# Router product inside the output projection, gated embedding tile by tile, three buffers of gathered rows

## What is computed

```python
# first block, after its four mixers have given y [512, 1024]
x1 = layer_norm(alpha * x + y @ w_out)                    # output projection
logits = x1 @ router_w + router_b                         # 32 experts
top_val, top_idx = top_k(logits, 4); gate = softmax(top_val)
# each token goes to its 4 experts (clamped SwiGLU), rows sorted by expert
ffn = alpha * x1 + sum_n gate[:, n] * expert_n(x1)
# gated embedding
h = ffn + sigmoid(ffn @ ple_gate_w) * (p @ ple_proj)
x  = layer_norm(layer_norm(h))                            # ln2, then ln_emb of the second block
# second block: two layers with retention, pooling and forgetting attention, and a feed-forward part
```

## Time and profile before

| | |
|---|---|
| median of 3 runs | 3852.95 us (3851.31 to 3853.45) |
| profiled execution, its time | 3862.78 us |
| its span, first to last instruction | 3861.0 us |
| mean granted PE clock | 0.892 of full |
| PE busy | 3518.7 us (91%) |
| DVE busy | 996.7 us (26%) |
| ACT busy | 445.7 us (12%) |
| POOL busy | 33.8 us (1%) |

### The profile page before, as it was taken

One profiled execution on the slowest core, in us unless ns is written; L12 is line 12 of the kernel. 1 busy time (PEld: TensorE's weight loads), 2 busy tenths in 40 slices (PEclk: granted clock), 3 DMA queues, 4 the chain that ended last, 5 costly groups with the idle time before them and its releaser, 6 DMA issues.

```text
span 3861.0 us, 52352 instructions
## 1 busy us (share of the span) xinstructions
PE 3518.7 (91%) x21886; PEld 2013.8 (52%) x21886; DVE 996.7 (26%) x2017; ACT 445.7 (12%) x990; POOL 33.8 (1%) x37
## 2 busy tenths in 40 slices
PE   8985578699999999999689889999999879999998
PEld 3553464444444444444346455888544646588843
DVE  0245764311111111111430354100021144300002
...
DMA packets 79323, 648.77 MB, mean 168 GB/s; under 512 B 8776, under 2 KB 21720, under 8 KB 45288
## 3 DMA queue, kind: packets, MB, share of 16 engines
...
## 4 chain that ended last, share of the span: by engine, by line
PE 88%; DVE 7%; issue 2%; DMA 2%; ACT 1%; POOL 1%; DVEq 0%; ACTq 0%; POOLq 0%; SPq 0%
PE psum L879 17%; PE psum L1225 16%; PE psum L1198 11%; PE psum L956 9%; PE psum L1025 5%; PE psum L545 4%; PE psum L553 3%; PE psum L1156 2%; PE psum L1043 2%; PE psum L561 2%; PE psum L1178 2%; PE psum L1083 2%; PE psum L1094 2%; PE psum L823 1%; PE psum L977 1%
## 5 line engine op out<-in xcount | busy, mean ns | idle before, releaser
L879 PE MATMUL psum<-weight_ring,arena 128*32 128x512 f32 x6192 | 685.1, 594 | 0.0
L1225 PE MATMUL psum<-arena,weight_ring 128*128 128x264 f32 x2816 | 627.1, 385 | 1.7 <-ACT arena L1617 1.7
L1225 PEld LDWEIGHTS psum<-arena,weight_ring 128*128 128x128 f32 x2816 | 532.2, 189 | 96.3 <-ACT arena L1617 2.2
L1198 PE MATMUL psum<-weight_ring,arena 128*128 128x512 f32 x960 | 414.1, 593 | 0.0
L879 PEld LDWEIGHTS psum<-weight_ring,arena 128*32 128x32 f32 x6192 | 195.3, 110 | 419.3 <-issue 406.7
L956 PE MATMUL psum<-weight_ring,arena 128*32 128x256 f32 x6144 | 338.2, 380 | 1.1
L545 PE MATMUL psum<-arena 128*128 128x128 f32 (+5 forms) x1078 | 187.8, 320 | 149.8 <-DVE arena L2302 24.7
L1198 PEld LDWEIGHTS psum<-weight_ring,arena 128*128 128x128 f32 x960 | 181.8, 190 | 232.6 <-issue 232.6
L545 PEld LDWEIGHTS psum<-arena 128*128 128x128 f32 (+5 forms) x1078 | 139.7, 167 | 272.3 <-issue 185.3
L956 PEld LDWEIGHTS psum<-weight_ring,arena 128*32 128x32 f32 x6144 | 196.5, 110 | 135.0 <-ACT arena L1574 8.7
L2221 DVE COPY arena<-psum 128x384 f32<-128x384 f32 x32 | 17.9, 561 | 808.8 <-PE psum L545 808.8
...
## 6 DMA issues: line engine op xcount, KB each, us to landing
...
y_sorted<-arena ACTq DMA_DIRECT2D x128, 96.0 KB, 10.8
...
```

The source lines that it names most:

```text
L879: mm = pe.matmul(psum[j * GROUP:(j + 1) * GROUP, g, :], xg[:, k, g * GROUP:(g + 1) * GROUP], w[:, kk, j * 512:(j + 1) * 512], start=(k == ...
L1198: mm = pe.matmul(bank[0:SIZE[t], :], lhs(k), rhs(k), start=(k == 0), stop=(k == tiles - 1))
L1225: mm = pe.matmul(bank[:, 0:HALF], w[:, k, at:at + P], h2_t[:, k, c * HALF:(c + 1) * HALF], start=(k == 0), stop=(k == KT - 1))
```

## The change

Three edits, each on several engines.

- **Router**: the tile's transposes and its 8 products of 32 columns move into `mix_out()`: after the second half's product group of tile 1 stands the routing of tile 0, after that of tile 2 the routing of tile 1, after that of tile 3 the routings of tiles 2 and 3. Each routing waits for its own two copies. The logits go to PSUM bank 7 instead of a bank of `v_ring`, with a semaphore of their own. On ACT the copies of x1's tile t - 1 stand behind the root of tile t.
- **Gated embedding**: all weights are waited for first; PE goes tile by tile, both halves of a tile together, and turns the next tile after the first half. ACT and DVE follow that order; the two norms of a tile come after its second half.
- **Gathered rows**: three buffers (slots 0 to 2) instead of two; POOL's wait for `ffn_ready` stands before the fourth tile only.

```diff
-        given_rows = ring[:, PIECE:3 * PIECE].rearrange("p (b n d) -> p b n d", b=2, n=TOP)
+        given_rows = ring[:, 0:3 * PIECE].rearrange("p (b n d) -> p b n d", b=3, n=TOP)
...
             for t in range(TT):
                 rwkv_tile(t)
-            def transposed_rows(source, ready):
-                for t in range(TT):
-                    if ready is not None:
-                        pe.wait_ge(ready, t + 1)
-                    for half in range(2):
-                        bank = a_ring.bank(pe)
-                        for k in range(4):
-                            mm = transpose(bank[:, k * P:(k + 1) * P], source[:, t, (4 * half + k) * P:(4 * half + k + 1) * P])
-                        job = a_ring.ship(mm)
+            def transposed_tile(source, t, ready=None):
+                if ready is not None:
+                    pe.wait_ge(ready, t + 1)
+                for half in range(2):
+                    bank = a_ring.bank(pe)
+                    for k in range(4):
+                        mm = transpose(bank[:, k * P:(k + 1) * P], source[:, t, (4 * half + k) * P:(4 * half + k + 1) * P])
+                    job = a_ring.ship(mm)
                 return job
+            def route_tile(t):
+                pe.wait_ge(a_ring.drained, transposed_tile(x1, t, sem("x1_ready")))
+                for k in range(KT):
+                    mm = pe.matmul(psum[:, 7, t * E:(t + 1) * E], x1_t[:, k, t * P:(t + 1) * P], router_w[:, k, :],
+                                   start=(k == 0), stop=(k == KT - 1), skip_group_check=True)
+                mm.then_inc(sem("logits_filled"), 1)
             def mix_out():
                 pe.wait_ge(sem("mixed"), 1)
-                pe.wait_ge(a_ring.drained, transposed_rows(y, None))
+                for t in range(TT):
+                    job = transposed_tile(y, t)
+                pe.wait_ge(a_ring.drained, job)
                 for half in range(2):
                     w = piece(7 + half)
                     for t in range(TT):
...
                         for k in range(KT):
                             mm = pe.matmul(bank, y_t[:, k, t * P:(t + 1) * P], w[:, k, :], start=(k == 0), stop=(k == KT - 1))
                         slot_free[7 + half] = (v_ring.filled, v_ring.ship(mm))
+                        if half == 1 and t == 1:
+                            pe.wait_ge(sem("router_landed"), 16 * 4)
+                        if half == 1 and t >= 1:
+                            route_tile(t - 1)
+                route_tile(TT - 1)
             def route():
                 before = CONST3(c3, "before")
                 routed = sem("routed")
-                pe.wait_ge(sem("router_landed"), 16 * 4)
-                pe.wait_ge(a_ring.drained, transposed_rows(x1, sem("x1_ready")))
-                bank = v_ring.bank(pe)
-                for t in range(TT):
-                    for k in range(KT):
-                        mm = pe.matmul(bank[:, t * E:(t + 1) * E], x1_t[:, k, t * P:(t + 1) * P], router_w[:, k, :],
-                                       start=(k == 0), stop=(k == KT - 1), skip_group_check=True)
-                v_ring.ship(mm)
                 pe.wait_ge(routed, 1)
                 bank = v_ring.bank(pe)
                 for t in range(TT):
...
                 return slot[(3 + n) % SLOTS]
             def gated_embedding():
-                pe.wait_ge(a_ring.drained, transposed_rows(ffn, sem("ffn_ready")))
-                for half in range(2):
-                    w = piece2(half)
-                    w_proj = piece2(2)
-                    for t in range(TT):
+                w = [piece2(n) for n in range(2)]
+                w_proj = piece2(2).rearrange("p k n -> p (k n)")
+                pe.wait_ge(sem("p_landed"), 16)
+                turned_job = transposed_tile(ffn, 0, sem("ffn_ready"))
+                for t in range(TT):
+                    pe.wait_ge(a_ring.drained, turned_job)
+                    for half in range(2):
                         bank = a_ring.bank(pe)
                         for k in range(KT):
-                            mm = pe.matmul(bank, h_t[:, k, t * P:(t + 1) * P], w[:, k, :], start=(k == 0), stop=(k == KT - 1))
-                        slot_free2[half] = (a_ring.filled, a_ring.ship(mm))
+                            mm = pe.matmul(bank, h_t[:, k, t * P:(t + 1) * P], w[half][:, k, :], start=(k == 0), stop=(k == KT - 1))
+                        a_ring.ship(mm)
                         bank = v_ring.bank(pe)
-                        if t == 0 and half == 0:
-                            pe.wait_ge(sem("p_landed"), 16)
                         for k in range(2):
-                            mm = pe.matmul(bank, p_t[:, k, t * P:(t + 1) * P],
-                                           w_proj.rearrange("p k n -> p (k n)")[:, k * D + half * 512:k * D + (half + 1) * 512],
+                            mm = pe.matmul(bank, p_t[:, k, t * P:(t + 1) * P], w_proj[:, k * D + half * 512:k * D + (half + 1) * 512],
                                            start=(k == 0), stop=(k == 1))
-                        slot_free2[2] = (v_ring.filled, v_ring.ship(mm))
+                        v_ring.ship(mm)
+                        if half == 0 and t + 1 < TT:
+                            turned_job = transposed_tile(ffn, t + 1, sem("ffn_ready"))
             mix_out()
             route()
...
                                             x1[:, t, :], None).then_inc(sem("scattered"), 16)
             pool.wait_ge(sem("all_stored"), 1)
             for t in range(TT):
-                if t >= 2:
-                    pool.wait_ge(sem("ffn_ready"), t - 1)
+                if t >= 3:
+                    pool.wait_ge(sem("ffn_ready"), t - 2)
                 for n in range(TOP):
                     at = TOP * t + n
-                    pool.indirect_dma_start(given_rows[:, t % 2, n, :], None, y_sorted,
+                    pool.indirect_dma_start(given_rows[:, t % 3, n, :], None, y_sorted,
                                             bass.IndirectOffsetOnAxis(ap=dest[:, at:at + 1], axis=0)
                                             ).then_inc(sem(f"given_rows_landed_{t}"), 16)
...
             rwkv_features()
             group_root(H)
-            def transposed_rows(out):
-                for t in range(TT):
-                    for half in range(2):
-                        bank = a_ring.take(act)
-                        A.did(act.copy(out[:, 4 * half:4 * half + 4, t * P:(t + 1) * P], bank.rearrange("p (k s) -> p k s", k=4)),
-                              a_ring.drained)
+            def transposed_tile(out, t):
+                for half in range(2):
+                    bank = a_ring.take(act)
+                    A.did(act.copy(out[:, 4 * half:4 * half + 4, t * P:(t + 1) * P], bank.rearrange("p (k s) -> p k s", k=4)),
+                          a_ring.drained)
             def route():
                 act.wait_ge(sem("gate_asked"), 1)
...
             def gated_embedding():
                 rows_root(A, 0, META)
-                transposed_rows(h_t)
-                mark["ple_gates"] = a_ring.taken
-                for n in range(2 * TT):
-                    bank = a_ring.take(act)
-                    if n >= TT:
-                        act.wait_ge(sem("gate_used"), n - TT + 1)
-                    A.did(act.activation(ple_gate[:, n % TT, :], bank, ACT.Sigmoid), a_ring.drained)
-                    if n >= TT:
-                        rows_root(A, n - TT)
-                        rows_root(A, n - TT)
-            transposed_rows(y_t)
+                mark["ple_gates"] = []
+                transposed_tile(h_t, 0)
+                for t in range(TT):
+                    for half in range(2):
+                        n = 2 * t + half
+                        bank = a_ring.take(act)
+                        if n >= TT:
+                            act.wait_ge(sem("gate_used"), n - TT + 1)
+                        A.did(act.activation(ple_gate[:, n % TT, :], bank, ACT.Sigmoid), a_ring.drained)
+                        mark["ple_gates"].append(a_ring.taken)
+                        if half == 0 and t + 1 < TT:
+                            transposed_tile(h_t, t + 1)
+                    rows_root(A, t)
+                    rows_root(A, t)
             for t in range(TT):
+                transposed_tile(y_t, t)
+            rows_root(A, 0)
+            for t in range(1, TT):
                 rows_root(A, t)
-            transposed_rows(x1_t)
+                transposed_tile(x1_t, t - 1)
+            transposed_tile(x1_t, TT - 1)
             route()
             experts()
             gated_embedding()
...
                     return v.rearrange("p t n e -> p t e n")
                 dve.wait_ge(sem("router_landed"), 16 * 4)
-                bank = v_ring.take(dve)
-                then(dve.tensor_tensor(logits, bank[:, 0:TT * E].rearrange("p (t e) -> p t e", t=TT),
```

(26 more changed lines are left out.)

## The result

| | before | after |
|---|---|---|
| median of 20 runs each | 3850.02 us (3842.56 to 3853.45) | 3855.4 us (3848.61 to 3858.24) |
| profiled execution | 3862.78 us, span 3861.0 | 3848.61 us, span 3846.8 |

The ratio is 1.0015, interval [1.0008, 1.0021]: the change costs 5.4 us where 1.4 were forecast as a gain. It is within 0.2% of no change, and inside the range, but the sign is wrong. The forecast also stood on a base that was too high: the median of the three runs was 3852.95, that of the twenty is 3850.02. The two profiled executions point the other way, since that of before lies above all of its 20 runs and that of after is the fastest of its 20. Two spans therefore can't be compared. Stages can, and only if one knows how much each varies by itself. That became the work of this study.

The account below looks back on a forecast made before the run. PE, busy 91% of the span, was taken as the main bound, with three affected places in series: router +5.8, gather -2.5, embedding -4.7, sum -1.4, from 3852.95 to 3851.5 us; eight times in ten 3843.0 to 3857.0.

Parts of the forecast that it names:

- router term: Router stage: moving the routings between wide product groups costs +5.8 us in all, ends -2.0 and +8.6.
- gather term: Gather stage: the third buffer of gathered rows brings -2.5 us, ends -4.9 and 0.
- Router, at full clock: Router stage if the clock stays full: it ends at 698.6 against 700.53 before, -2.0 us.
- Router, the clock: Router stage: two clock falls and a half-clock last routing turn -2.0 into +5.8 us.
- put each fall at 2.0: Router stage: each of two clock falls behind a routing costs 2.0 us, slightly over 1.7; ends 0 and 3.4.
- 0.91 says that the engines were full: Gather stage: DMA engines at 0.91 of their time make transfers the limit, so -2.5 us was taken.
- the third buffer moves no landing: Rival, gather stage: transfers were the limit all along, term 0, time 3854.0 us, no change; chance 0.1.
- Gated embedding: Gated embedding stage: going tile by tile, it ends at 1951.6 instead of 1956.24, -4.7 us; ends -6.4 and -2.
- bank-wait rival: Rival, gated embedding: PE waits 1.3 us at each tile for a bank, not 0.1; 3855.0 us; chance 0.07.
- Sum: Whole kernel: router, gather and embedding together, +5.8 - 2.5 - 4.7 = -1.4 us, so 3851.5 us.
- The clock does not fall: Rival, router stage: the clock stays full, term -2.0 us, time 3843.7 us, faster; chance 0.13.
- wide groups don't bring it back: Rival, router stage: the clock stays low through tiles 2 and 3, +13.2 us, time 3864.7; chance 0.05.

Follow-up runs that it names:

- r4: The changed kernel with all three edits, run again against the kernel before: 3864.82 us against 3862.44, ratio 1.0004 [0.9995, 1.0014].
- r12: The changed kernel with all three edits, run again in a later series against the kernel before: 3848.93 us against 3848.85, ratio 1.0003 [0.9994, 1.0012].

## Why the prediction was wrong

Three steps failed. The router term was too small, since each fall of the clock cost more than the 2.0 put for it and the base was one bad case. The gather term, a gain, was too small as well. And the stages that the edits don't touch had no term. The first two errors cancel, so they do not explain the sign; the third may.

**Router, at full clock.** Right in its parts: pauses of 2.76 (2.7 forecast), transposes 1.04 (1.0), narrow products 1.97 at full clock (1.7, too low by 0.3 each).

**Router, the clock.** The mechanism was right: two falls, each ended by the group behind it, and a last routing at half clock. The step that failed is "put each fall at 2.0", with the base that the sum was made against. Each fall cost 2.75: the two wide groups lost 4.5 together (9.75 + 8.81 - 2 x 7.03), and the narrow products of two routings 1.0. Some came back behind the last wide group, where 11.9 us passed and not the 12.6 worked out. Against the profile of before the stage grew by 6.7, not 5.8. The larger error is the base: 84.0 was one of the worst cases of the old order. Ten profiles of it average 82.9 (79.3 to 84.1), four of the new one 90.8, all within 0.1. The edit costs 7.9 on average because it also takes away the good case, in which the clock outlasts part of the narrow products. I had read one fall, at 683, as a property of the code. The Trainium skill (TensorE: Matmul & The Clock Gate, A second HAM failure mode: psum-queue depth-cycling) names the failure, and the trace agrees: a throttle at each routing, 90.8 against 83.1 with the pauses filled.

**Gathered rows.** I took -2.5 from the 322 GB/s and the share of 0.91; measured is -4.7 (36.5 to 31.8, means of 7 and 13 profiles), near the end of -4.9 at which DVE works without a gap. What failed is "0.91 says that the engines were full". That rate is a mean over 13 us that begin with the first packets: in before the engines moved 298 GB/s from 1830 to 1834 and 396 from 1838 to 1842, and in after, while the third tile was gathered, 406 at a share of 1.01. The rows of tiles 1 and 2 then came before DVE needed them, and those of tile 3 only 0.69 late. POOL issues 512 KB each 1.24 us, which asks for 423 GB/s, near what was moved, so the runs do not separate issue from transfer as the limit. The Trainium skill's fit for a transfer issued by POOL (DMA: Bandwidth & Descriptors, Anatomy of one DMA — SWDGE (gpsimd) path) had given -4.9, and the trace agrees with it here. The rival "the third buffer moves no landing" is out.

**Gated embedding.** -4.7 forecast, -3.8 measured on average (91.8 to 88.0), -4.3 in the first pair of profiles. The early start, the cold start (8.56 for 7.03, so 1.5 against 1.7 forecast) and the tail of 10.05 stand as forecast; the bank waits are 0.5 in all against 0.2. The bank-wait rival is out.

**Sum.** 7.9 - 4.7 - 3.8 = -0.6, near the forecast's -1.4, but by luck, since an error of +2.1 (router) and one of -2.2 (gather) cancelled. Measured were +5.4, +2.4 (r4) and +0.1 (r12), +2.6 on average, and only the first is clear of no change. The prediction had no term for a stage that it didn't touch. One such stage leans the wrong way: the rest is 1908.7 on average in the twelve profiles with both later edits and 1906.1 in the other eight. With these 2.7 the sum would be +2.1. That is an estimate from single profiles, and that the edits cause it is not shown. For the +5.4 of the first series the record has one hint more. The three fastest of the 20 runs of after (3848.61 to 3851.62) had a mean granted clock of 0.895, the other 17 (3853.96 to 3858.24) 0.892 to 0.894, and the fastest, the profiled one, has the short case. The other 17 may have had the long one, about 5 us more. No profile shows it, and none shows how often before had it, so the sign of the first result stays open.

**Rivals.** "The clock does not fall" and "wide groups don't bring it back" are both out: it fell three times, and came back within both wide groups. The order interleaved as said.
